# First attention: inverse sums of the near units multiplied into the result through a diagonal product

## The reference, cut to what matters

```python
qkv = hn @ na_wqkv                      # q and k are then normalised per head, with gains
s_loc = einsum(q_row, k_win) * scale + bias          # latent queries, keys nearby
s_ctx = einsum(q_row, kc) * scale                    # latent queries, context keys
p = softmax(concatenate([s_loc, s_ctx], axis=-1))    # one sum for both parts
out = einsum(p_loc, v_win) + einsum(p_ctx, vc)
# the context's own queries see the context keys alone
y = out @ na_wo;  h = h + gate * y
```

## Time and profile before

| | us |
|---|---|
| three timed runs | 2732.64, 2738.05, 2738.17 |
| median of them | 2738.05 |
| profiled execution, its span from first to last instruction | 2732.2 |
| PE busy in the span | 2622.8 (96%) |
| DVE, ACT, POOL busy | 1546.6, 1073.3, 875.4 |

### The profile page before, as it was taken

How to read it: one execution, slowest core, us unless ns; L and a number is a source line. 1 busy time by engine, 2 the same in 40 slices (tenths; PEclk the granted TensorE clock), 3 DMA queues, 4 the chain that set the end, 5 groups by cost and what they waited for, 6 DMA issues and landing times. The chain is left out here.

```text
span 2732.2 us, 38254 instructions
## 1 busy us (share of the span) xinstructions
PE 2622.8 (96%) x14748; PEld 2130.9 (78%) x14748; DVE 1546.6 (57%) x2893; ACT 1073.3 (39%) x1864; POOL 875.4 (32%) x651
## 2 busy tenths in 40 slices
PE   6899999999999999999889999999999999999997
PEld 4777786788888888766668888787778888788886
DVE  4434344687777778556664444544556445516555
ACT  4454545422222222565542322344553434542222
POOL 1211121243333333021124444333334333444443
PEclk8999999999999999999999999999999999999999
DMA  6323333223332332110012222322212221222221
GB/s 244 116 79 97 107 99 115 85 96 108 106 107 107 108 108 70 57 47 32 32 47 96 104 92 92 96 66 74 78 47 102 71 85 62 94 93 93 93 93 62
DMA packets 69652, 243.02 MB, mean 89 GB/s; under 512 B 11780, under 2 KB 29700, under 8 KB 49288
## 3 DMA queue, kind: packets, MB, share of 16 engines
q1 hardware_dynamic: 69512, 241.15, 25.8%
HBM read 239.02 MB, written 2.10 MB: 88 GB/s over the span
## 5 line engine op out<-in xcount | busy, mean ns | idle before, releaser
L248 POOL TENSOR_TENSOR w_lo<-w_raw,w_hi 128x512 fp32r<-128x512 f32 x612 | 820.2, 1371 | 1736.7 <-ACT w_hi L241 602.9
L287 PE MATMUL bank<-u_hi,w_hi 128*128 128x512 f32 (+1 forms) x1952 | 731.8, 375 | 10.8 <-DVE u_lo L547 5.0
L289 PE MATMUL bank<-u_hi,w_lo 128*128 128x512 f32 (+1 forms) x1952 | 719.4, 369 | 0.0
L288 PE MATMUL bank<-u_lo,w_hi 128*128 128x512 f32 (+1 forms) x1952 | 718.7, 368 | 0.0
L287 PEld LDWEIGHTS bank<-u_hi,w_hi 128*128 128x128 f32 x1952 | 368.9, 189 | 80.9 <-issue 14.0
L288 PEld LDWEIGHTS bank<-u_lo,w_hi 128*128 128x128 f32 x1952 | 368.9, 189 | 62.2 <-issue 2.5
L289 PEld LDWEIGHTS bank<-u_hi,w_lo 128*128 128x128 f32 x1952 | 368.5, 189 | 62.3
L1052 DVE SCALAR_TENSOR_TENSOR resid<-bank,mod,resid 128x512 f32<-128x512 f32 (+1 forms) x384 | 242.0, 657 | 140.5 <-PE bank L289 136.1
L287 PE MATMUL bank<-hid_hi,w_hi 128*128 128x512 f32 (+1 forms) x768 | 275.5, 359 | 0.0
L289 PE MATMUL bank<-hid_hi,w_lo 128*128 128x512 f32 (+1 forms) x768 | 273.0, 355 | 0.0
L288 PE MATMUL bank<-hid_lo,w_hi 128*128 128x512 f32 (+1 forms) x768 | 272.1, 354 | 0.0
(11 more groups left out here) (410 smaller groups left out, 3888.6 us busy)
## 6 DMA issues: line engine op xcount, KB each, us to landing
w_raw<-stream SPq DMA_DIRECT2D x150, 1024.0 KB, 4.9
w_raw<-stream SPq DMA_DIRECT2D x56, 512.0 KB, 4.4
ada_ring<-stream SPq DMA_DIRECT2D x48, 512.0 KB, 4.7
bias<-bias SPq DMA_DIRECT2D x192, 64.0 KB, 2.3
ada_more<-stream SPq DMA_DIRECT2D x6, 1024.0 KB, 13.2
resid<-h SPq DMA_DIRECT2D x2, 1536.0 KB, 8.7
w_raw<-stream SPq DMA_DIRECT2D x8, 256.0 KB, 3.9
out<-resid SPq DMA_DIRECT2D x8, 256.0 KB, 2.0
```

What stands on the lines that cost most here:

```text
L248: ins = eng.tensor_tensor(m.wl[:, s, w], m.raw[:, s, w], m.wh[:, s, w].bitcast(F32), ALU.subtract)
L287: pe.matmul(out, lh, rh, start=start, stop=False)
L288: pe.matmul(out, lh, rl, start=False, stop=False)
L289: return pe.matmul(out, ll, rh, start=False, stop=stop)
```

## The change: what it does, and the diff

For the near units `exps` are left as they are. `turn(G)` waits for `exps(G)` and no longer for a multiplication. DVE makes the reciprocals of the sums and, for each head, a 128 x 128 diagonal matrix of them (`shares`: the identity times the reciprocals). PE, at the end of `weigh(G)`, multiplies a 128 x 64 matrix of ones with that diagonal, for both heads, into the second bank of the set: every row of the product then holds the 128 reciprocals. DVE copies it to SBUF (`share`) and multiplies it into the result in PSUM (`normalise_y`); `high_y(G)` waits for that. The context units are done as before.

DVE's order is now: `maximum(G+1)`, `shares(G)`, `low_y(G-1)`, the copy of the chunk's result, `gated`, at t = 3 `normalise_context(G+1)`, `normalise_qk`, `normalise_y(G)`, more. `low_y` thus runs one unit later than it did.

```diff
--- before.py
+++ after.py
@@ -1384,6 +1384,7 @@
         e = sb("e", [P, 2, LOC + CTX])
         pt = sb("pt", [P, 2, LOC + CTX])
         stat = sb("stat", [P, 2, 16])
+        diag, share = sb("diag", [P, 2, P]), sb("share", [P, P])
         norm = Apply(m, m.rstd, TOK, lambda k, w: m.gsc[:, 0, 0, k, w:w + 1],
                      lambda k, w: m.mod[:, 0, 0, k, w:w + 1],
                      [pt[:, 0, :], pt[:, 1, :], s_sb[:, :, :].rearrange("p h n -> p (h n)")], by_columns=True)
@@ -1398,7 +1399,9 @@
         bias_in, bias_last_in = count("bias_in"), count("bias_last_in")
         lin_done, lin_free = count("lin_done"), [count("lin_free0"), count("lin_free1")]
         squared, rstd_done, qk_done = count("squared"), count("rstd"), count("qk_normed")
-        scored, turned, weighed, maxed, exped, copied, inverted, normed = (m.shared(n) for n in PER_UNIT)
+        scored, turned, weighed, maxed, exped, copied, inverted = (m.shared(n) for n in PER_UNIT[:-1])
+        shared_out, share_read, y_normed, context_normed = (
+            count("shared_out"), count("share_read"), count("y_normed"), count("context_normed"))
         max_parts, summed = count("max_parts"), count("summed")
         y_high, set_free = count("y_high"), count("set_free")
         lin = Linear(m, (0, 1), lin_done, lin_free)
@@ -1463,6 +1466,10 @@
 
         def banks(G):
             return m.bank[:, 2 + 2 * (G % 3):4 + 2 * (G % 3), :]
+
+        def near_count(G):
+
+            return NEAR * groups[G][0] + groups[G][1] + 1
 
         def half(hd):
             return slice(DH * hd, DH * hd + DH)
@@ -1640,7 +1647,7 @@
 
                 def high_y(G):
                     i, t = groups[G]
-                    act.wait_ge(*weighed.at(G + 1))
+                    act.wait_ge(*(y_normed.at(near_count(G)) if t < NEAR else weighed.at(G + 1)))
                     if t < NEAR:
                         ins = act.activation(grid(yh[:, i % 4, 0:LAT])[:, :, 16 * t:16 * t + 16],
                                              columns_as_rows(banks(G)[:, 0, 0:P]), ACT.Copy)
@@ -1733,25 +1740,36 @@
                     dve.scalar_tensor_tensor(out=st[:, 4:6], in0=st[:, 0:2], scalar=-1.0, in1=st[:, 2:4],
                                              op0=ALU.mult, op1=ALU.min).then_inc(maxed.sem)
 
-                def normalise(G):
-                    i, t = groups[G]
+                def shares(G):
+
                     st = stat[:, G % 2, :]
                     dve.wait_ge(*exped.at(G + 1))
-                    if t < NEAR:
-                        dve.tensor_tensor(st[:, 8:10], st[:, 8:10], st[:, 10:12], ALU.add).then_inc(summed.sem)
-                        dve.wait_ge(*summed.at(NEAR * i + t + 1))
-                        dve.reciprocal(st[:, 12:14], st[:, 8:10]).then_inc(inverted.sem)
-                        dve.wait_ge(*inverted.at(G + 1))
-                        for hd in range(2):
-                            x = e[:, hd, local(t).start:LOC + CTX]
-                            ins = dve.tensor_scalar(x, x, st[:, 12 + hd:13 + hd], None, ALU.mult)
-                    else:
-                        dve.reciprocal(st[:, 12:16], st[:, 8:12]).then_inc(inverted.sem)
-                        dve.wait_ge(*inverted.at(G + 1))
-                        for q in range(4):
-                            x = e[:, q // 2, q % 2 * CTX:q % 2 * CTX + CTX]
-                            ins = dve.tensor_scalar(x, x, st[:, 12 + q:13 + q], None, ALU.mult)
-                    ins.then_inc(normed.sem)
+                    dve.tensor_tensor(st[:, 8:10], st[:, 8:10], st[:, 10:12], ALU.add).then_inc(summed.sem)
+                    dve.wait_ge(*summed.at(near_count(G)))
+                    dve.reciprocal(st[:, 12:14], st[:, 8:10]).then_inc(inverted.sem)
+                    dve.wait_ge(*inverted.at(G + 1))
+                    if G:
+                        dve.wait_ge(*weighed.at(G))
+                    for hd in range(2):
+                        ins = dve.tensor_scalar(diag[:, hd, :], cst(m, "ident"), st[:, 12 + hd:13 + hd], None, ALU.mult)
+                    ins.then_inc(shared_out.sem)
+
+                def normalise_context(G):
+                    st = stat[:, G % 2, :]
+                    dve.wait_ge(*exped.at(G + 1))
+                    dve.reciprocal(st[:, 12:16], st[:, 8:12]).then_inc(inverted.sem)
+                    dve.wait_ge(*inverted.at(G + 1))
+                    for q in range(4):
+                        x = e[:, q // 2, q % 2 * CTX:q % 2 * CTX + CTX]
+                        ins = dve.tensor_scalar(x, x, st[:, 12 + q:13 + q], None, ALU.mult)
+                    ins.then_inc(context_normed.sem)
+
+                def normalise_y(G):
+                    y = banks(G)[:, 0, 0:P]
+                    dve.wait_ge(*weighed.at(G + 1))
+                    dve.tensor_copy(share[:, :], banks(G)[:, 1, 0:P]).then_inc(share_read.sem)
+                    dve.wait_ge(*share_read.at(near_count(G)))
+                    dve.tensor_tensor(y, y, share[:, :], ALU.mult).then_inc(y_normed.sem)
 
                 def low_y(G):
                     i, t = groups[G]
@@ -1788,11 +1806,14 @@
                 for p in range(QK):
                     normalise_qk(0, p)
                 maximum(0)
-                normalise(0)
                 for G, (i, t) in enumerate(groups):
                     j = i + 1
                     if G + 1 < len(groups):
                         maximum(G + 1)
+                    if t < NEAR:
+                        shares(G)
+                    if G:
+                        low_y(G - 1)
                     if G in chunk_at:
                         n = use["ada", chunk_at[G][1]]
                         dve.wait_ge(*lin.ready(n))
@@ -1800,11 +1821,12 @@
                     kind, x = beside.get(i, ("-", 0))
                     for y in parts(i, t)[0] if kind == "wo" else ():
                         gated(x, y)
-                    if G + 1 < len(groups):
-                        normalise(G + 1)
+                    if t + 1 == NEAR:
+                        normalise_context(G + 1)
                     if t == 1 and j < PAIRS:
                         normalise_qk(j, 0)
-                    low_y(G)
+                    if t < NEAR:
+                        normalise_y(G)
                     if t == 1 and j < PAIRS:
                         normalise_qk(j, 1)
                         normalise_qk(j, 2)
@@ -1818,6 +1840,7 @@
                         if c % 24 // 4 in (1, 4):
                             dve.wait_ge(*lin.read(n))
                             mod_gain(dve, m, c)
+                low_y(len(groups) - 1)
                 for x in range(4):
                     gated(3, x)
                 split_lo(dve, m, 1, 1)
@@ -1929,7 +1952,7 @@
                 def turn(G):
                     i, t = groups[G]
                     s = banks(G)
-                    pe.wait_ge(*normed.at(G + 1))
+                    pe.wait_ge(*(exped.at(G + 1) if t < NEAR else context_normed.at(i + 1)))
                     for hd in range(2):
                         if t < NEAR:
                             for b, ((x, y), _, _) in enumerate(LOCAL[t]):
@@ -1956,8 +1979,12 @@
                         for b, (tile, keys) in enumerate(blocks):
                             for hd in range(2):
                                 r = half(hd)
-                                ins = pe.matmul(s[r, 0, 0:P], vp[keys, tile, r], pt[keys, hd, b * P:b * P + P],
-                                                start=(b == 0), stop=(b == 3))
+                                pe.matmul(s[r, 0, 0:P], vp[keys, tile, r], pt[keys, hd, b * P:b * P + P],
+                                          start=(b == 0), stop=(b == 3))
+                        pe.wait_ge(*shared_out.at(near_count(G)))
+                        for hd in range(2):
+                            ins = pe.matmul(s[half(hd), 1, 0:P], cst(m, "ones")[:, 0:DH], diag[:, hd, :], start=True,
+                                            stop=True)
                     else:
                         for b in range(2):
                             for hd in range(2):
@@ -2019,7 +2046,7 @@
                     output(3, x)
                 after.sum(pe, [(m.lin[1][:, a:b], lambda t, a=a, b=b: t[:, a:b]) for a, b, _ in spans(TOK)])
                 keep_busy(pe, m, m.bank[:, 4, :], 2)
-        for name in PER_UNIT:
+        for name in PER_UNIT[:-1]:
             m.spent(name, len(groups))
     finish_stage(m, 3 * PAIRS, 0)
     return after
```

## The result

The changed kernel took 2746.78 us in the median of 7 runs (2742.19 to 2750.03), the kernel before 2735.68 in 7 runs of the same session (2732.64 to 2742.48). The ratio is 1.003 (95% interval 1.0017 to 1.0043), so it is slower by about a third of a per cent, 11.1 us by these medians. The profiled execution has a span of 2741.0 us against 2732.2, 8.8 us more.

A forecast was written before the change was run, and what follows sets the result against it. PE, busy for 96% of the span, was taken as the bound. The terms 7.2 - 0.8 - 0.25 - 0.1 - 0.1 + 0.9 + 1.95 + 0.2 gave +9.0 us, median 2738.05 to 2747.0, range 2739 to 2755.

The forecast's parts named there:

- PE is the bound, and what is added to its queue is paid: Whole kernel: PE is busy for 96% of the span, so work added to its queue costs its full time.
- 0.225 us a unit, the heads side by side: Weighing of 32 near units: the added matmuls of both heads overlap, 0.225 us a unit, 7.2 us in all.
- Unit 0: -0.8: Turn of unit 0: it can start about 0.8 us earlier, as the exponentials end sooner.
- The chunk's copy: +0.9, +1.0 and +1.0: Units 1, 12 and 22: DVE's added work delays the chunk's copy and PE behind it, +0.9 and twice +1.0 us.
- The multiplication of the result costs nothing: Near units: the high result starts 0.6 us after the weighing, but this is covered; without cover 0.4 us three times.
- Units 2 to 4: -0.25 beyond their matmuls: Turns of units 2 to 4: gains and new delays nearly cancel, -0.25 us beyond the added matmuls.
- Diagonals beside POOL: DVE's queue: reciprocals, diagonals and low part add 1.0 us, between 0.6 and 1.8 us, the latter with POOL at work.
- The waits for DVE as the most a quicker normalising can give: PE's turns: any quicker normalising can give at most about 5.2 us, the waits for DVE's normalised exponentials.
- not slower: Turns and stretches at half clock: 5.2 us of waits and 3.4 us go, in sum -1.4 us, 2736.7; chance 17%.
- one after another: Added matmuls on PE: the two heads do not overlap, 14.1 us in place of 7.2, in all +15.9; chance 8%.
- waits for the diagonal in units with a fill: Two dozen units with a fill: PE waits at most 1 us each for late diagonals, +20 or more; chance 2%.
- the queue delays: DVE and chunk queues: POOL's slowing, uncovered chunk chain and more half-clock stretches cost more, +14.5 us, 2752.5; chance 21%.

The follow-up runs named there:

- the two doses: Changed kernel without the diagonal's two matmuls, and with them done twice; medians 2740.93 and 2753.95 us, 6.5 us a dose.
- copy_first: Changed kernel with DVE's copy of the chunk's result ahead of the diagonals and the low part of the unit before; ratio 1.0033 to the kernel before.
- no_product: Changed kernel without the diagonal's two matmuls and PE's wait for the diagonal; ratio 1.0012 to the kernel before.
- product_twice: Changed kernel with each of the diagonal's two matmuls done twice; ratio 1.006 to the kernel before.
- the second profile: Changed kernel run and profiled once more with nothing altered; ratio 1.0032 to the kernel before, first scores to last weighing 426.43 us.
- no_normalising: Kernel before without the near units' multiplication of the exponentials, their turns waiting for the exponentials; ratio 0.9999 to the kernel before.
- after_high_copy: Changed kernel with the chunk's copy ahead of the diagonals and the weights' high part directly behind the copy of the transposes; ratio 1.0011 to the kernel before.

## Why the prediction was right

The forecast was 2747.0 us and +9.0 for the stage; measured were 2746.78 and +8.15. That the medians agree to 0.2 us is luck. The forecast stood on 2738.05, the median of three runs, and seven runs of the kernel before gave 2735.68. By the medians the growth was 11.1 us here and 8.0 in the later session, against 9.0 forecast. The direction, the bound and the order of the size are what was right. The steps one by one:

- *PE is the bound, and what is added to its queue is paid.* Shown by the two doses: 0.22 us in each unit with a fill, no more and no less.
- *0.225 us a unit, the heads side by side.* Measured 0.22. The rule of the Trainium skill's page "TensorE: Matmul & The Clock Gate", section "The mechanism", by which the sum would have been 6.9 us higher, is not borne out by the two doses: the second pair of matmuls, with the column halves of one row group like the first, cost two steps and not four.
- *Unit 0: -0.8.* Right (-0.75 with the matmuls' 0.22 in it, so -0.97).
- *The chunk's copy: +0.9, +1.0 and +1.0.* Right in place and releaser. `copy_first` gives 0.57, 0.75 and 0.99 of it back. Beside the matmuls unit 1 cost 0.56, so less than forecast, and units 12 and 22 cost 1.0 and 1.2.
- *The multiplication of the result costs nothing.* Right in most units with projection; units 13, 22 and 23 paid 0.12 to 0.25 us. For units 9, 19 and 29 the cover fell short: the chunk came 0.68, 0.55 and 0.55 us later and PE itself only 0.44. I had also put the exposure at 0.4 each; it is 0.5.
- *Units 2 to 4: -0.25 beyond their matmuls.* They gave -1.06 us in all, -1.5 beyond the matmuls, and this is the largest miss in the sum. It is the clock. Unit 4 alone gave -1.47: it does the same matmuls, but in the kernel before its weighing and the scores behind it ran at half the clock (rows below). All six profiles of the changed order without a half-clock stretch in unit 4 took 4.28 us for it. The two with one, `no_product` and `product_twice`, took 5.9. Units 2 and 3 together gave +0.41 for their 0.44 of matmuls, and +0.18 in the second profile, where no stretch was near. So the waits were sized about right, and what the sum lacked was a term for a stretch that comes or goes.

```profile
135.27 1.98 PE L1965 MATMUL bank<-pt,v 128*64 128x256 f32 x8 [1.11 <-ACT pt L1639]
...
134.25 1.08 PE L1992 MATMUL bank<-pt,v 128*64 128x256 f32 x8 [1.11 <-ACT pt L1646]
```

- *Diagonals beside POOL.* The bound of 1.8 us for `shares` and `low_y(G-1)` was too low, as rows 6 had shown only a partial meeting. Beside POOL the two diagonals alone take 2.3 us. They meet in ten units (3, 8, 10, 15, 18, 20, 25, 28, 30, 33). In eight of these PE has a fill and never waits for the diagonal. It waits 0.5 us in unit 3 and 1.2 in unit 33, and 0.4 and 1.0 in units 2 and 32, where the diagonals were not slowed but PE has no fill. Of these four waits, 3.1 us in all, the forecast had named only unit 2's. They did not show in the sum, as the turns behind them wait no more.
- *The waits for DVE as the most a quicker normalising can give.* True as a bound (5.2), useless as an estimate: `no_normalising` gave nothing that the timed runs show. That weighs against the rival "not slower" too: in the changed kernel near turns wait no more for DVE, and yet of three half-clock stretches in the stage one went (10.2 us at half clock before, 6.8 now) and the others moved.
- The gap between span and stage (-1.48 ahead, +2.2 behind) was not predicted at all. With it the span grew by 8.8 us against 9.0 forecast, which again is better than the steps deserve: errors of up to 1.5 us cancel, and single runs spread by 8 to 10 us.

The rivals: one after another is shown false; waits for the diagonal in units with a fill do not exist; the queue delays came out at the forecast's price, not at the rival's 14.5. Its mechanism of POOL slowing the diagonals is real (it stands behind PE's waits in units 3 and 33), and an earlier `high` makes it cost more.

## What to carry to other kernels

Where one engine is full, moving a division from idle engines' time to two short matmuls costs those matmuls in full (7 us here), and the new order on the other engines costs more where a bank has no slack (2.8 us here). What it saves in waits has to be looked for behind each wait: here only unit 0's was a gain, and the others turned into the next wait. A gain of 1.5 us in one unit can be the clock's, so compare the times of the same matmuls before it is called the change's. A copy that frees a bank should stand ahead of work that only the unit's end needs. Before a step is moved ahead, lay its followers' time (here POOL's, through `high`) beside the short operations of the other engines.

## What the runs showed of the hardware

A DVE multiplication by a scalar, SBUF to SBUF in float32, that begins while a POOL instruction is in flight ends a little after that instruction: 0.08 to 0.09 us for 128 columns, 0.15 for 256, 0.25 for 448 and 0.28 to 0.29 for 512. That is 0.2 us less than each takes when quiet, so most of its time is the rest of POOL's instruction. In the changed kernel's 64 diagonals, 44 took 0.28 us in the median, and the 20 that met POOL 1.01 to 1.33, with POOL's own four taking about 1.25 each. In the kernel before, the 448 and 512 columns of line 1747 took 0.45 and 0.48 when quiet and 1.24 and 1.28 beside POOL.

Sums of two values in SBUF behave alike: four of the changed kernel's sums of two columns (line 1747) began with over 0.1 us of such an instruction left, took 0.19 to 1.20 us in place of 0.15, and ended 0.02 us after it. Not slowed were the reciprocal (line 1749, 0.17 us in ten meetings), and what reads PSUM: the low part (line 1783, 0.28 us in five meetings) and the first addition to the residual (line 1794, 0.75 us in nine). The copy of the reciprocals (1770) and the product (1772) never met POOL in that run; in `after_high_copy` they did twice and kept their 0.29 and 0.30 us. Timelines of DVE and POOL, quiet and not:

```profile
224.76 0.48 DVE L1754 TENSOR_SCALAR diag<-cst_sb,stat 128x128 f32<-128x128 f32 x2
...
127.60 2.30 DVE L1754 TENSOR_SCALAR diag<-cst_sb,stat 128x128 f32<-128x128 f32 x2
...
126.08 4.97 POOL L248 TENSOR_TENSOR w_lo<-w_raw,w_hi 128x512 fp32r<-128x512 f32 x4 [31.14 <-ACT w_hi L1584]
```

The Trainium skill names a likely reason: its page "GPSIMD Engine Reference", section "Specifications", has GpSimd share its SBUF interfaces with VectorE, with contention for VectorE instructions in a 2-port mode or with two SBUF inputs. The traces agree as to which instructions are hit as far as they show it: the sums with two SBUF inputs were, the reciprocal with one and those that read PSUM were not. That the cause is the shared interface was not tested by itself.

A wait on PE that is already fulfilled cost nothing measurable. In the 28 units in which the diagonal was ready, its first matmul started 0.102 or 0.103 us after the weighing's last, with the wait between them, and the weighing's own steps without one are the same 0.102 or 0.103 us.
